# Expert rows packed by rank in shares of 32 to 160, and the last layer's expert outputs summed on TensorE

## What is computed

```python
N_EXPERTS, TOP_K, D_EXPERT, D_SHARED = 64, 8, 256, 256

def routed_experts(xf, eidx, wts, w_g, w_u, w_d):      # xf: tokens x 1024, eidx: tokens x 8
    ...                                                # the rows of each expert, in blocks of 128
    yb = swiglu(xb, w_g[e], w_u[e], w_d[e])            # (silu(xb @ w_g) * (xb @ w_u)) @ w_d
    y = yb.reshape(-1, D)[dest]
    y = y * wts.reshape(-1)[order][:, None]
    return jnp.zeros((N, D), y.dtype).at[tok].add(y)

def moe_ffn(xf, ...):
    ...                                                # 8 of 64 experts for each token, by sigmoid scores
    return routed + swiglu(xf, w_s_gate, w_s_up, w_s_down)
```

## Time and profile before

| | us |
|---|---|
| median of three runs | 2765.43 (2758.46 to 2767.33) |
| profiled execution | 2772.11 |
| its span in the profile | 2770.3 |
| PE busy in it | 2492.9 (90%) |
| units of layer 0, first to last but one | 920 to 1502 |
| units of layer 1, first to last but one | 2196 to 2689 |
| end of layer 1's last such unit to end of span | 82 |

### The profile page before, as it was taken

The page is one execution under the profiler, slowest core; times in us unless marked ns, Lnnn a source line. Parts: engine busy times, 40 slices in busy tenths (PEclk is TensorE's granted clock), DMA queues, the critical chain, the costliest instruction groups (busy, mean ns, idle before and its releaser), DMA issues.

```text
span 2770.3 us, 38767 instructions
## 1 busy us (share of the span) xinstructions
PE 2492.9 (90%) x15920; PEld 1401.6 (51%) x15920; DVE 820.1 (30%) x1966; ACT 597.5 (22%) x1190; POOL 170.2 (6%) x178
## 2 busy tenths in 40 slices
PE   8999798999998999899899799978999898788886
PEld 4466377644446444344344557657888532233334
DVE  1455445311117121111111525455311521111113
ACT  4444313200021111111111244233202011111111
POOL 0000000000000111111111000000000111111110
PEclk9999899999996999999999899999999799989997
DMA  7100142321004599999997731031340899999993
GB/s 311 71 8 31 61 154 97 150 73 79 31 0 197 213 370 422 391 414 400 372 411 281 293 126 65 31 117 69 128 153 27 321 383 425 423 418 417 410 399 157
DMA packets 74704, 616.34 MB, mean 222 GB/s; under 512 B 17694, under 2 KB 17822, under 8 KB 32160
## 3 DMA queue, kind: packets, MB, share of 16 engines
q1 hardware_dynamic: 50336, 563.47, 49.9%
q0 software_dynamic: 24192, 50.39, 4.8%
HBM read 603.82 MB, written 47.71 MB: 235 GB/s over the span
## 4 chain that ended last, share of the span: by engine, by line
PE 83%; DVE 6%; issue 4%; DMA 4%; ACT 2%; SPq 0%; POOLq 0%; ACTq 0%; DVEq 0%; POOL 0%
PE bank L1856 22%; PE bank L1871 10%; PE bank L1338 9%; PE bank L300 6%; PE bank L1353 3%; PE bank L1343 3%; PE bank L392 3%; PE bank L1846 3%; DMA arena<-expert_rows 2%; PE bank L1034 2%; PE bank L1049 2%; PE bank L317 1%; PE bank L469 1%; PE bank L446 1%; PE bank L1051 1%
## 5 line engine op out<-in xcount | busy, mean ns | idle before, releaser
L1856 PE MATMUL bank<-ring,arena 128*64 128x512 f32 (+1 forms) x1648 | 588.4, 633 | 101.1 <-issue 96.2
L1856 PEld LDWEIGHTS bank<-ring,arena 128*64 128x64 f32 (+1 forms) x1648 | 203.6, 159 | 424.4 <-issue 423.4
L1338 PE MATMUL bank<-normed,ring 128*128 128x512 f32 (+1 forms) x768 | 255.5, 486 | 0.0
L1856 PE MATMUL bank<-branches,arena 128*64 128x512 f32 (+1 forms) x528 | 249.2, 628 | 0.0
L2046 DVE TENSOR_TENSOR arena<-bank,arena 128x256 f32<-128x256 f32 x83 | 35.2, 424 | 705.9 <-ACT arena L1965 705.9
L1780 POOL DMA_INDIRECT arena<-hidden_rows,block_slots x81 | 82.3, 1016 | 2158.5 <-DVE block_slots L1605 1552.1
L1338 PEld LDWEIGHTS bank<-normed,ring 128*128 128x128 f32 x768 | 145.9, 190 | 101.8 <-issue 91.8
L1965 ACT ACTIVATE arena<-bank 128x256 f32<-128x256 f32 x83 | 31.9, 384 | 688.1 <-PE bank L1856 688.1
L1871 PE MATMUL bank<-ring,arena 128*64 128x512 f32 (+1 forms) x560 | 163.4, 597 | 1.3 <-DVE arena L2052 1.3
L300 PE MATMUL bank<-normed,ring 128*128 128x512 f32 (+1 forms) x416 | 160.2, 544 | 0.0
L1871 PE MATMUL bank<-arena 128*64 128x512 f32 (+1 forms) x528 | 139.9, 604 | 1.1 <-ACT arena L1968 1.1
(11 more groups left out here) (442 smaller groups left out, 3319.8 us busy)
## 6 DMA issues: line engine op xcount, KB each, us to landing
ring<-in_wexp SPq DMA_DIRECT2D x96, 2048.0 KB, 19.2
ring<-in_wst SPq DMA_DIRECT2D x54, 2048.0 KB, 8.5
branches<-in_wexp SPq DMA_DIRECT2D x34, 2048.0 KB, 22.3
ring<-in_wexp SPq DMA_DIRECT2D x66, 1024.0 KB, 22.1
arena<-in_wexp SPq DMA_DIRECT2D x64, 1024.0 KB, 21.4
arena<-expert_rows SPq DMA_DIRECT2D x9, 2048.0 KB, 11.2
branches<-expert_rows SPq DMA_DIRECT2D x3, 2048.0 KB, 16.2
ring<-in_wst SPq DMA_DIRECT2D x2, 1536.0 KB, 19.4
```

Source lines behind the costliest of these rows:

```text
L1338: last = nc.tensor.matmul(ps[2 * (n % 4)][:, c0:], wg[:, k, i * P:(i + 1) * P], H[:, k, c0:], start=(k == 0), stop=(k == KD - 1))
L1856: last = nc.tensor.matmul(ps[2 + s][r0:r1, :], XT_[:, s, k * P + r0:k * P + r1], wt[:, k, :], start=(k == 0), stop=(k == KD - 1))
```

## The change

1. **Packing.** `Packed` replaces `Plan`. A place has 32, 64, 96, 128 or 160 rows, and places lie one behind the other, so that a unit holds up to four places. A unit is cut into pieces of 128, 64 or 32 rows; if any border in it is not at 0 or 64, all pieces have 32 rows. Layer 0 has 43 units (13 of them in 32-row pieces), layer 1 has 27 (14 in 32-row pieces).
2. **Layer 1 has its own unit code** (`ex_sync`, `ex_pool`, `ex_pe`, `ex_act`, `ex_dve`). Output rows are not stored. They are scaled by the choice's weight when they leave PSUM, and PE adds them to the tokens by a matmul with a one-hot matrix (8 matmuls, 256 columns) into four PSUM banks that are kept through the whole layer. The weights go to DRAM once and are gathered by index, 4 bytes a row, one gather a unit. The shared expert's down product is made first, into the same banks. All weights have a fifth slot (`normed` and a piece of `arena`). Expert 0's down weights are loaded only after that product.
3. **Routing arithmetic** (`place_rows`) is written for contiguous rows; `choice_weights` of layer 1 runs ahead of unit 0 in place of within units 3 to 5. The final norm uses another bank.

```diff
-PLAN = (Plan(0, "FFDP" * 2 + "FFP" * 4 + "P" + "FFP" * 5 + "P" + "FFP" * 4), Plan(4, "PPPDPD" + "P" * 28))
+    SHARES = {"A": (64, 64), "B": (64, 32, 32), "C": (96, 32), "D": (128,), "F": (128,), "E": (160, 96), "G": (96, 96, 64)}
...
+            n = 32 if any(r0 % 64 or r1 % 64 for r0, r1, q in of) else P if len(of) == 1 else 64
+            units.append([(r, r + n, q) for r0, r1, q in of for r in range(r0, r1, n)])
...
+        loads = [(self.last_use[q - slots] + late, self.last_use[q - slots], kind, q)
+                 for q in range(slots, E - 2) for kind, late in (("gate_up", 0), ("down", 1.3))]
...
+PLAN = (Packed(0, 4, "AAFFFAGAFAAGEAFEGGAFGGGEGGGAAA"), Packed(4, 5, "AABAABADCBCABBABBBAABABCBAA"))
...
-                    for r0, r1, p in sides(unit):
+                    for r0, r1, p in unit:
```

The new order on PE in layer 1, with the combining matmul:

```diff
+            def combine(s):
+                for m in range(KD):
+                    last = nc.tensor.matmul(acc(m), YB[s][:, m * P:(m + 1) * P], OH[s], start=False, stop=False)
+                return last
...
+            for u in range(U):
+                rows_through(u)
+                if u + 1 < U:
+                    flip_left(u + 1)
+                if u:
+                    rows_down(u - 1)
+                if u + 1 < U:
+                    flip_right(u + 1)
+                pe.wait_ge(un["dve"], after_last("dve", "hidden", u))
+                flip_hidden(u % 2, tl["pe"] if u == freed_by + 1 else None).then_inc(un["pe"], 1)
+                if u >= 2:
+                    to_tokens(u - 2)
...
+            def weigh(u):
+                if u >= 4:
+                    pool.wait_ge(*weight_arrived(u - 4))
+                pool.indirect_dma_start(SW[:, u:u + 1], None, wrow, bass.IndirectOffsetOnAxis(ap=ids_of[:, u, 1:2], axis=0), bounds_check=TX * TOPK - 1, oob_is_err=False).then_inc(y_out[u % 4], 16)
```

More of the change, by code:

```diff
@@ L39 @@
 NOBODY = 8192.0
[L42 to L62, removed]
-        self.n = len(units) + NOV // 2 + 1
[L64 to L70, removed]
@@ new lines, with __init__ @@
+class Packed:
+    SHARES = {"A": (64, 64), "B": (64, 32, 32), "C": (96, 32), "D": (128,), "F": (128,), "E": (160, 96), "G": (96, 96, 64)}
+    def __init__(self, pinned, slots, order):
+        cap = [rows for what in order for rows in self.SHARES[what]]
+        start = [sum(cap[:q]) for q in range(E)]
+        units = []
+        for u in range(sum(cap) // P):
+            of = [(max(start[q], P * u) - P * u, min(start[q] + cap[q], P * (u + 1)) - P * u, q) for q in range(E)]
+            of = [(r0, r1, q) for r0, r1, q in of if r0 < r1]
+            n = 32 if any(r0 % 64 or r1 % 64 for r0, r1, q in of) else P if len(of) == 1 else 64
+            units.append([(r, r + n, q) for r0, r1, q in of for r in range(r0, r1, n)])
+        assert len(cap) == E and units[-1] == [(0, 64, E - 2), (64, P, E - 1)]
+        self.pinned, self.all, self.units, self.start, self.cap = pinned, units, units[:-1], start, cap
+        self.n = len(units) + NOV // 2 + 1
+        self.by_rank = list(range(pinned)) + sorted(range(pinned, E), key=lambda q: (-cap[q], q))
+        self.last_use = [(start[q] + cap[q] - 1) // P for q in range(E)]
+        loads = [(self.last_use[q - slots] + late, self.last_use[q - slots], kind, q)
+                 for q in range(slots, E - 2) for kind, late in (("gate_up", 0), ("down", 1.3))]
@@ L1666, in build @@
                  "dve": (("silu", 0), ("hidden", 0), ("rows", 1), ("out", -1))}
+        LAST_STEPS = {"pe": (("gate_up", 0), ("flip_left", 1), ("down_left", -1), ("down_right", -1), ("flip_right", 1), ("flip_hidden", 0), ("combine", -2)),
+                      "act": (("sigmoid", 0), ("rows", 1), ("out", -1), ("hidden", 0)),
+                      "dve": (("silu", 0), ("hidden", 0), ("out", -1), ("rows", 1), ("one_hot", -1))}
         COUNT, total = {}, {"pe": 0, "act": 0, "dve": 0}
         for _l in range(L):
-            for _eng, _steps in STEPS.items():
-                for _u in range(-1, len(PLAN[_l].units) + 1):
+            for _eng, _steps in (STEPS if _l == 0 else LAST_STEPS).items():
+                for _u in range(-1, len(PLAN[_l].units) + 2):
                     for _name, _off in _steps:
```

485 lines of the change are left out of this document (424 added, 61 removed).

## The result

| | before | after |
|---|---|---|
| median | 2765.78 us (four runs) | 2671.02 us (four runs, 2668.90 to 2675.02) |
| profiled execution | 2772.11 us | 2670.35 us |
| its span | 2770.3 us | 2668.2 us |

The ratio is 0.9664, 95% interval 0.9643 to 0.9685. The median fell by 94.8 us, where 77 were forecast.

The account below looks back on a forecast made before the run. The prediction took PE and DMA as nearly level in layer 0's expert stage and DMA as the bound in layer 1's. Savings of 40 + 13 + 24 = 77 us from 2765.4 gave 2688 us, 8-in-10 range 2664 to 2716.

Parts of the forecast that it names:

- What bounds the stages: Expert stages: layer 0 has PE and DMA nearly level and turns DMA-bound; layer 1 is paced by the DMA engines alone.
- 534 us plus 4 idle: Layer 0's stage: DMA work plus idle time make 538 us against 578, 40 us less, bounds 25 and 46.
- Layer 1's static stage: Layer 1 to its last static gate and up: stores go, down weights and weight gathers add; 13 us less.
- My last rival: More gain than summed: layer 1's DMA rate rises to 421 GB/s, 12 us, plus 6 in layer 0; below 2665; chance 0.05.
- Layer 1 keeps 1.00 with four slots: Layer 1's DMA share in the kernel before, cited as evidence that loads would not come late.
- the rival that loads come late: Both expert stages: DMA engines don't stay full, the 77 us gain falls to 47, 2718 us; chance 0.12.
- PE as cover: Layer 1's stage: 26 units of 15.5 us make 403 us on PE against 473 of DMA, 70 us slack.
- Four 32-row pieces: Layer 0 on PE: four pieces run side by side, 0.3 us more a unit, 4 us for 13 units.
- my first rival: Four pieces cost more than two: PE's 534 us equal the DMA's 534 in layer 0, about 18 us, 2706; chance 0.12.
- The tail: Layer 1 from the last static gate and up to the end: 57.8 us in place of 81.7, 24 us less.
- Routing arithmetic: `place_rows` ahead of the units has about as many DVE operations as it replaces: 0, within 1 us.
- The signs: Expected trace marks: layer 0 DMA share at least 0.99, layer 1 at 1.00, more PE gaps in layer 0, 32-row steps 0.43 us.

Follow-up runs that it names:

- experiment 2: Changed kernel with layer 0 cut into 49 units again, in contiguous rows, layer 1 as changed: 2719.9 us.
- experiments 6 and 12: Changed kernel with layer 1's output-row stores put back: 2690.5 us; and changed kernel with row gathers only for layer 1's first three units and the loop: 2647.4 us.
- experiment 8: Changed kernel with one of the eight combining matmuls a unit in layer 1: 2656.6 us.
- experiment 4: Changed kernel with layer 0's same 43 units reordered, the first twelve using one expert each: 2692.7 us.
- experiment 7: Changed kernel with only the first four weight gathers in layer 1, 22 left out: 2665.8 us.
- experiment 5: Changed kernel with four slots for weights in layer 1 in place of five: 2697.4 us.
- experiment 9: Changed kernel with every combining step of layer 1's static units made twice: 2709.2 us.
- experiment 10: Changed kernel with every static unit of both layers cut into four 32-row pieces: 2681.1 us.
- experiment 3: Changed kernel with three pair units of layer 0 turned into six wide units, 46 in place of 43: 2686.2 us.

## Why the prediction was right, and where its sums were off

- **What bounds the stages** held. Layer 0 passed from PE to the DMA engines (share 1.00; experiment 2 gives it back), layer 1 stayed with them (experiments 6 and 12 move it by 23 and 24 us for 8.4 and 7.3 MB; experiment 8 takes 69.5 us of PE work out of it for 3.9).
- **Layer 0: 47 us where 40 were summed.** The term "534 us plus 4 idle" was too large: the queues' shares over the stage are 84.7% and 14.7% of 531, 528 us, and about 2 were idle. My 534 came from the stretch 920 to 1500 us, which also held weights that the DMA engines loaded ahead while PE was late; when they are the bound, these fall behind the stage's end: q1 carried 188.8 MB in the stage before and 187.2 after, 1.6 MB or 4 us less, while q0 has 30.9 in both. The upper bound of 46 was 1 us short. That early units which bring few new experts leave the DMA engines idle, and that this isn't made up, is shown by experiment 4: 17 us back by order alone.
- **Layer 1's static stage: 33 us where 20.4 were summed.** The later start of unit 0 is in both numbers. From the end of the mixer, which leaves it out, it is 25 us where 13 were summed, and four terms make up the 12. The weight gathers were put at 5 us and cost 1 to 1.5 (experiment 7, for 26). Expert 0's down weights were counted as +2.6, but q1 carried 199.6 MB in both kernels. Idle time of 3 us that went was not in the sum. The stores, 20.4 in the sum, took 19.4 us of the engines and 23.4 of the stage when put back. I also wrote that the fifth slot's loads would keep the DMA engines busy ahead of unit 0. They were issued as it started; what moved ahead of it are place 3's 3 MB.
- **The DMA rate** rose in layer 1 from 411 to 417 GB/s. My last rival had 421 for it, 12 us, and 6 more in layer 0. Of that, about half came in layer 1 (460 x 6 / 417 = 6.6 us, an estimate that overlaps the terms above) and 7 in layer 0. By its own terms it stood at 2688 - 18 = 2670, not below 2665, and 2671 was measured: its chance of 0.05 looks too small.
- **"Layer 1 keeps 1.00 with four slots"** was my evidence against the rival that loads come late. It was no evidence: with 27 units four slots lose 23.4 us, nearly all of it idle time (experiment 5). That row came from a kernel with 34 units of at most two experts. Layer 1's part of the forecast held only because the change also brings the fifth slot, and the rival deserved more than the weight I gave it in the argument, though it didn't come true.
- **PE as cover** held, with less to spare than I wrote. 403 us of PE work were forecast and 401 measured, but the 70 us of slack were against 473 us of DMA work, and the stage took 460: PE was idle for 59. Experiment 9 could cover 57.5 us of added work, 12.7 of them by the higher clock.
- **Four 32-row pieces** cost nothing: steps of 0.43 us, 7.00 us in all, and 0 in experiment 10; the 0.3 us a unit that I added in layer 0 was not there. The Trainium skill ("TensorE: Matmul & The Clock Gate", section "Measured speedup vs the span model") has 2.38 for three column tiles; by an estimate from that, a group would take 3 / 2.38 = 1.26 of a single one. Here a group of four takes 7.00 / 6.87 = 1.02 of a step of 128 rows, and the measurement decides.
- **That two nearly level resources cost extra** was in my first rival, priced at 18 us for the wrong cause. Experiment 3 has 10 us, 3 of which are its order of units. With 43 units PE was busy for 500 us and the DMA engines for 528, and their share was 1.00.
- **The tail: 22.3 where 24 were summed**, 59.1 us for 57.8. The loop's down product took 5.35 us in place of 3.7.
- **Routing arithmetic** moved layer 0's start by +0.7 us, less than that start varies from run to run. Nothing spilled: each loop ran once.
- **The signs** came out: shares of 1.00, layer 0's last static gate and up ending at 1452.3 for 1459, layer 1's units 17.7 us apart for 18, and 59.1 us behind them for 58. PE's gaps ahead of gate and up in layer 0 became more (10 in place of 3), but not longer in all (22.8 us for 21.3).

## What to carry to other kernels

When a resource is called full, ask in which slices, and what was in them: a mean over a stage that another engine bounds overstates the work that the stage must wait for. A change that shortens one engine's part also changes how far ahead loads must be let go; price the buffers again with the new units, since a share of 1.00 under the old ones says nothing. And where PE and the DMA engines have equal work, don't expect the longer of the two: here 529 and 528 us made 541, while 500 and 528 made 531.

## What the runs showed of the hardware

- The DMA engines held 411 to 420 GB/s from HBM for 430 to 530 us on end, in a kernel on one core; a stretch of 6.3 us (2603.7 to 2610.0 us in experiment 8) showed 436, at a share of 1.03, so short windows count a little too much. The Trainium skill ("DMA: Bandwidth & Descriptors", section "Where 436 GB/s comes from") gives 435 as the ceiling of the ports, and no stage here is above it; it lets some 358 bind for transfers from HBM, and every stage here is above that.
- A gather of 128 x 4 bytes showed 32 packets and about 0.02 us of the sixteen engines' time; 22 of them lengthened the stage by 0.7 to 1.3 us.
- Gate and up behind a gap of 4 us took 8.5 us in place of 7.0, at a granted clock of 0.83, between the two levels of 1.2 and 2.4 GHz.
- Between the stages, the same instructions took 696.7 to 710.1 us (689.6 without the shared product), with the granted clock low at more or fewer places. This is larger than the 0.3% that I took as the noise, and what decides it stays open.
